# Tiles of the normed x laid 1040 bytes apart instead of 1024, in a two-layer hybrid decoder kernel

## The reference

```
h = RMSNorm(x);  p = h @ w_in            # 2048 -> q | k | v | z | xBC | dt
A = sliding-window attention(q, k, v)    # 16 heads of 64, window 128, sinks, ALiBi
S = Mamba-2 mixer(z, xBC, dt)            # conv, SiLU, chunked scan, gate, grouped RMSNorm
x = x + concat([A, S]) @ w_out
x = x + (silu(RMSNorm(x) @ w_gate) * (RMSNorm(x) @ w_up)) @ w_down   # width 5632
```

## The kernel before, in words

| tensor | address | home of its tiles |
|---|---|---|
| `w_hi`, `w_lo` | 33280, 50176 | 0 |
| `w_hi_s`, `w_lo_s` | 33344, 50240 | 64 |
| `xr` (x itself) | 67072 | 0 |
| `h_hi`, `h_lo` | 83456, 99840 | 0, all 16 tiles |
| `wdt_s` | 130624 | 64 and 192 in turn |
| `f_hi`, `f_lo`, `m_hi`, `m_lo` | from 138240 | 0 |

## Time and profile before

### The profile page before, as it was taken

The page is one execution under the profiler, slowest core; times in us unless marked ns, Lnnn a source line. Parts: engine busy times, 40 slices in busy tenths (PEclk is TensorE's granted clock), DMA queues, the critical chain, the costliest instruction groups (busy, mean ns, idle before and its releaser), DMA issues.

```text
span 2156.1 us, 33054 instructions
## 1 busy us (share of the span) xinstructions
PE 2143.3 (99%) x14202; PEld 1941.3 (90%) x14202; DVE 1198.6 (56%) x1360; ACT 1001.7 (46%) x1250; POOL 112.7 (5%) x157
## 2 busy tenths in 40 slices
PE   9999999999999999999999999999999999999999
PEld 7888888999999999888888887899999999998887
DVE  5866665555555555544467666555555555554443
ACT  5555655444444444434445556544444444443332
POOL 2023110000000000000000222000000000000000
PEclk9999999999999999999999999999999999999999
DMA  7554356666666666565656544566666666666664
GB/s 219 176 166 131 122 173 177 201 192 193 194 195 196 193 193 193 189 196 190 190 164 184 156 123 127 182 186 194 191 194 195 195 195 192 192 194 204 204 197 137
DMA packets 202882, 392.69 MB, mean 182 GB/s; under 512 B 12224, under 2 KB 12592, under 8 KB 202736
## 3 DMA queue, kind: packets, MB, share of 16 engines
q1 hardware_dynamic: 201952, 388.67, 59.9%
q0 software_dynamic: 784, 1.90, 0.4%
HBM read 388.43 MB, written 2.10 MB: 181 GB/s over the span
## 4 chain that ended last, share of the span: by engine, by line
PE 98%; ACT 1%; issue 0%; POOL 0%; SPq 0%; DMA 0%; DVE 0%; DVEq 0%; ACTq 0%
PE ps L501 47%; PE ps L689 44%; PE ps L510 2%; PE ps L603 1%; PE ps L552 0%; PE ps L667 0%; PE ps L666 0%; PE ps L639 0%; PE ps L640 0%; PE ps L665 0%; POOL ys L468 0%; DMA vrows<-in_k_norm_w_dram 0%; PE ps L608 0%; PE ps L611 0%; PE ps L594 0%
## 5 line engine op out<-in xcount | busy, mean ns | idle before, releaser
L689 PE MATMUL ps<-h_hi,w_hi_s 128*128 128x256 f32 x2816 | 779.4, 277 | 0.0
L689 PE MATMUL ps<-h_hi,w_lo_s 128*128 128x256 f32 x2816 | 779.2, 277 | 0.0
L689 PE MATMUL ps<-h_lo,w_hi_s 128*128 128x256 f32 x2816 | 779.1, 277 | 0.0
L1079 DVE TENSOR_TENSOR w_lo<-raw,w_hi 128x1024 fp32r<-128x1024 f32 x384 | 476.0, 1243 | 381.7 <-ACT w_hi L839 380.5
L1079 DVE TENSOR_TENSOR w_lo_s<-raw,w_hi_s 128x1024 fp32r<-128x1024 f32 x352 | 431.1, 1225 | 437.1 <-ACT w_hi_s L839 437.1
L839 ACT CAST w_hi_s<-raw 128x1024 fp32r<-128x1024 f32 x352 | 369.5, 1050 | 527.5 <-PE ps L689 512.1
L839 ACT CAST w_hi<-raw 128x1024 fp32r<-128x1024 f32 x384 | 403.5, 1051 | 424.8 <-PE ps L501 406.7
L689 PEld LDWEIGHTS ps<-h_hi,w_hi_s 128*128 128x128 f32 x2816 | 529.3, 188 | 0.1
L689 PEld LDWEIGHTS ps<-h_lo,w_hi_s 128*128 128x128 f32 x2816 | 529.0, 188 | 0.1
L689 PEld LDWEIGHTS ps<-h_hi,w_lo_s 128*128 128x128 f32 x2816 | 528.8, 188 | 0.0
L501 PE MATMUL ps<-w_hi,f_hi 128*128 128x512 f32 x960 | 297.7, 391 | 0.0
(11 more groups left out here) (195 smaller groups left out, 1011.4 us busy)
## 6 DMA issues: line engine op xcount, KB each, us to landing
raw<-in_w_gate_dram SPq DMA_DIRECT2D x176, 512.0 KB, 3.7
raw<-in_w_up_dram SPq DMA_DIRECT2D x176, 512.0 KB, 3.6
raw<-in_w_down_dram SPq DMA_DIRECT2D x176, 512.0 KB, 4.7
raw<-in_w_in_dram SPq DMA_DIRECT2D x144, 512.0 KB, 3.6
raw<-in_w_out_dram SPq DMA_DIRECT2D x64, 512.0 KB, 4.7
out_dram<-xr SPq DMA_DIRECT2D x4, 512.0 KB, 6.4
xr<-in_x_dram POOLq DMA_DIRECT2D x3, 512.0 KB, 6.2
xr<-in_x_dram SPq DMA_DIRECT2D x1, 512.0 KB, 4.5
```

Of the source, the lines that this page charges most:

```text
L689: done = nc.tensor.matmul(ps[:, bank + m // 2, m % 2 * TOK:(m % 2 + 1) * TOK], w[:, slot, k, m * P:(m + 1) * P], h[:, rows + k, :], start= ...
L1079: v_.tensor_tensor(lo[:, slot, :, :], raw[:, slot, :, :], hi[:, slot, :, :].bitcast(F32), ALU.subtract).then_inc(lo_split, 1)
```

## The change

The rows of `h_hi` and `h_lo` get four floats more per tile, which nothing reads or writes: views cut them off again. Tile k now starts 1040·k bytes from its tensor's start. To make room, the unused gap behind `w_lo` shrinks from 512 to 128 bytes, which moves everything from `xr` to `den`: `xr`, `h_hi` lie 384 bytes lower, and what comes behind `h_lo` 128 bytes higher. `w_hi`, `w_lo`, their shifted overlays and everything from `f_hi` on stay.

```diff
         w_lo = sb("w_lo", [P, RING, 2, N], F32R, 512)
-        sb("w_lo_gap", [P, P])
+        sb("w_lo_gap", [P, P // 4])
...
         xr = sb("xr", [P, T, D], F32, 128)
-        h_hi = sb("h_hi", [P, KT, TOK], F32R, 128)
-        h_lo = sb("h_lo", [P, KT, TOK], F32R, 128)
+
+        h_hi = sb("h_hi", [P, KT, TOK + 4], F32R, 128)[:, :, 0:TOK]
+        h_lo = sb("h_lo", [P, KT, TOK + 4], F32R, 128)[:, :, 0:TOK]
```

## The result

The changed kernel takes **2198.57 us** (median of 2 runs, 2198.09 to 2199.06) where 2157.2 stood before: ratio 1.019, 95% interval 1.0171 to 1.0208. It is slower by 41 us, and my forecast and my range (2152 to 2180) are both wrong. From here on a **difference** is the home of the weights minus the home of h, modulo 256; before, it was 64 on line 689 and 0 on line 501 for `w_in`. The experiments move them again: `w_in` is on line 501, 502, 503 or 516, gate and up on 689, 690, 691, 694 or 705.) One of the ten runs of the experiment that puts the weights of `w_in` back had a granted clock of 0.71 and took 2842.52 us; its ratio is that of the other nine.

The account below looks back on a forecast made before the run. PE, busy for 99% of the span, was taken as the bound, so only the matmul pace could matter. All terms were 0: span 2156.1 + 0 = 2156.1 us, 2157.2 against the median; range 2152 to 2180.

Parts of the forecast that it names:

- The step that failed: Matmuls reading h on lines 689, 501 and 552: three known homes show one pace, so the pace change is 0 us.
- The sign that I had set for being wrong: Line 689: a pace that goes by the tile number, k from 0 to 15, would refute the forecast.
- −79 and +53 us: All matmuls reading h: −79 us if each runs a column a cycle, +53 us if each falls to the slow pace.
- The two paces at one set of homes: Line 689: 117.8 ns until `spread_rs`, 113.34 ns after, at homes that did not differ; entered by how the stream before ended.
- By the column, not by the byte: bf16 streams with half the bytes a column also lose the sixteenth, which speaks against a quarrel over addresses.
- Rival B: Nearly all matmuls reading h fall to the slow pace, as the walk prevents locking: +53 us, 2210 us; chance 0.05.
- Rival A: Matmuls reading h: each of 992 steps of home upsets the lock, about 0.02 us each, +20 us, 2177; chance 0.31.
- C: Lines 689 and 501: the lost sixteenth is a collision of homes that walking breaks, −59 us, 2098; chance 0.06.
- D: Slow stretches shaken loose (−2.0 us) and shorter settling behind small work (another 2 to 4 us): 2151 to 2155; chance 0.11.
- The rule on the pace: Back-to-back matmuls start N ÷ 2.4 GHz plus about 2.5 ns apart: line 689 at 109.2 ns, line 501 at 215.8.
- The rule on the ports: PE's stream and weight load have read ports of their own, so no difference of homes costs anything: 0 us.
- Zero for x, stage and the other moved tensors: Loads, stores and other engines at shifted addresses: 0 us, with ±1 us kept for the range.

Follow-up runs that it names:

- The maps: Against the kernel before: h at one home (0, then 128), weights' home stepped 16 bytes per chunk or `w_in` group, 2212.52 and 2211.71 us; with h at 0, 4-byte steps, 2211.57.

## Why the prediction was wrong

*What bounds the kernel.* Right: PE, and its pace alone. But for the 0.8 us of a low clock at the start of the profiled execution, the extra time is in the pace of the matmuls that read h.

*The step that failed*: "I take 0, since the three homes of the rows lie nearest to it." The three were one difference each for three different loops: 0 on line 501, 64 on line 689, 64 and 192 on line 552. I read them as points of one curve. The maps show that each loop has its own list: on line 689 a difference of 0 runs at 120.0 ns, though line 501 is at its best there. Line 552, which I took as showing that a change of home is free, slowed down itself, from 114.4 to 118.1 ns. For line 689 I had a single point, 64, and it happened to be the one difference of 16 that is always fast in the maps. The sign that I had set for being wrong, a pace that goes by the tile number, is what the trace shows. A range bounded at −79 and +53 us with one point inside deserved no strong middle.

*The two paces at one set of homes.* I took them as evidence against homes. They are what difference and entry make together: the difference sets which states exist, and what ran before sets which one is taken. The same holds at 192, 113.3 or 117.8, and at 76, 113.4 or 120.0. Which entry leads to which state, no run explains.

*"By the column, not by the byte."* It was a fair reading of the earlier trace rows and says something about the sixteenth that is always lost, which no difference touched. It says nothing about the second, larger loss, and I let it count against both.

*The bounds and the rivals.* +37.7 us was my upper end for line 689 and 34.1 came; for `w_in` 15.4 and some 5.8. Rival B had the mechanism, a walk that keeps the stream from locking; I gave it 0.05 and asked four fifths of the matmuls for 43 us, and nearly that happened. That its price fits as well is luck: it took 117.8 for every matmul, and what came is 113.3 to 120.0 by the tile, with a mean of 117.6. Rival A's step costs 22 to 32 ns at difference 64 where I had put 20, but A alone, with fast tiles between the steps, is not what took place. C and D did not come about.

*The rule on the pace.* The Trainium skill, "TensorE: Matmul & The Clock Gate", section "Wait — 56ns, not 53.3ns?", would let line 689 run at 109.2 ns. None of the differences tried came below 113.3, so the rows stand against it here.

*The rule on the ports.* The same page's section "Step-by-step: what each phase is for" has separate read ports for the stream and the weight load, so that one takes no bandwidth from the other. The run that moved PE's stream address alone, 454.3 to 473.5 us, doesn't fit that: for `float32r` operands the pace depends on the difference of the two reads' addresses, so that they do get in each other's way. Whether it is bandwidth that one takes from the other, no run shows.

*Zero for x, stage and the other moved tensors*: right, shown by 0.9999 with `w_in`'s difference restored.

## What to carry to other kernels

When PE is busy for 99% of the span, take the pace of its main loops from long pieces of the chain and compare it between loops; then treat the difference between the addresses of what is loaded and what is streamed as a tuning parameter of each loop, and map it in one run by letting it change from block to block. Once a loop runs at its best pace, keep the difference constant through the loop: an edit elsewhere that moves one operand by 128 bytes can cost it, and so can a stride that varies the home. A single good point in the trace doesn't say that its surroundings are good. And a map of held differences doesn't tell the pace of a walk through them, as 144 shows; what a walk costs has to be measured.

## What the runs showed of the hardware

The pace of `float32r` matmuls with 256 columns depends on the difference of the two operands' addresses in steps of one element, with a period of 256 bytes: from 113.3 ns (three of the 22 differences between 44 and 128) to 122.2. With 512 columns `w_in` went from 226.7 to 232.4 ns for a difference of 128, and at 28 it was at its pace at once after an interruption, where at 0 it took up to ten matmuls. At some differences two steady states exist (64, 192 and 76), and the state changed over two transposes from the slow to the fast one (64) and from the fast to the slow one (76); that the transposes did it is the likely reading, no run took them out. The granted clock was 1.00 in all of these stretches. What within PE or the memory collides, and why none was faster than 17/16 of a column a cycle, is open.
